# A latent attention lead-in in another order: the first four output tiles of the recurrent group stand ahead of head 0's projections, and the value weights are rounded behind head 0's squares

## The reference

```python
ob_l = mlstm_output(hb_l, pl[6], ml_head_gain[l])
...
q = (rms_norm(p[8], gq) @ w_uq).reshape(B, T, MLA_HEADS, MLA_NOPE + MLA_ROPE)
kv = (rms_norm(p[9], gkv) @ w_ukv).reshape(B, T, MLA_HEADS, MLA_NOPE + MLA_V)
k_nope, v = kv[..., :MLA_NOPE], kv[..., MLA_NOPE:]
...
q = rms_norm(q, qk_gain[0])
k = rms_norm(jnp.concatenate([k_nope, k_rope], axis=-1), qk_gain[1])
...
mix_l = jnp.concatenate([flat_heads(oa_l), ob_l, flat_heads(oc_l)], axis=-1) @ w_out[l]
```

## Time and profile before

| | |
|---|---|
| median of 3 runs | 2276.22 us (2275.09 to 2277.04) |
| the profiled execution: time, span | 2275.96 us, 2274.2 us |
| granted TensorE clock, mean over the span | 0.974 |
| TensorE matmul busy | 2104.3 us (93%) |
| VectorE, ScalarE, GpSimd busy | 1183.4, 751.0, 641.6 us |

### The profile page before, as it was taken

How to read it: one execution, slowest core, us unless ns; L and a number is a source line. 1 busy time by engine, 2 the same in 40 slices (tenths; PEclk the granted TensorE clock), 3 DMA queues, 4 the chain that set the end, 5 groups by cost and what they waited for, 6 DMA issues and landing times.

```text
span 2274.2 us, 30058 instructions
## 1 busy us (share of the span) xinstructions
PE 2104.3 (93%) x11774; PEld 1735.1 (76%) x11774; DVE 1183.4 (52%) x2119; ACT 751.0 (33%) x1221; POOL 641.6 (28%) x820
## 2 busy tenths in 40 slices
PE   6887999988889999999999988889988889999999
PEld 4576888866667888888888867778866658878887
DVE  4467613558874667166526566662358864212212
ACT  4234223456653311111111233322355644212222
POOL 1200311220002233333333421131221004555555
PEclk9999999999999999999999999999899989999999
DMA  7300332110002233233323210010111002223223
GB/s 283 102 7 32 120 116 83 38 37 19 10 10 66 75 112 121 84 112 112 102 94 120 85 57 19 19 58 29 47 38 37 10 10 71 96 93 97 97 93 102
DMA packets 76242, 165.58 MB, mean 73 GB/s; under 512 B 5192, under 2 KB 46664, under 8 KB 75088
## 3 DMA queue, kind: packets, MB, share of 16 engines
q1 hardware_dynamic: 75728, 163.28, 21.4%
q10 hardware_dynamic: 384, 0.47, 0.1%
HBM read 161.63 MB, written 2.10 MB: 72 GB/s over the span
## 4 chain that ended last, share of the span: by engine, by line
PE 79%; DVE 9%; ACT 5%; issue 5%; POOL 1%; DMA 1%; PEld 0%; SPq 0%; PEldq 0%; DVEq 0%; ACTq 0%; POOLq 0%
PE psum L1054 22%; PE psum L1056 21%; PE psum L1055 21%; PE psum L1613 1%; DVE naptlo L1986 1%; POOL wlo L517 1%; PE psum L1253 1%; PE psum L1136 1%; PE psum L1162 1%; DMA wm<-w_mod 1%; PE psum L1105 1%; PE psum L1382 1%; PE psum L1368 1%; PE psum L1319 1%; PE psum L1194 1%
## 5 line engine op out<-in xcount | busy, mean ns | idle before, releaser
L517 POOL TENSOR_TENSOR wlo<-raw,whi 128x256 fp32r<-128x256 f32 x816 | 641.4, 817 | 1624.5 <-ACT whi L542 1624.5
L1054 PE MATMUL psum<-hhi,whi 128*128 128x512 f32 (+1 forms) x1640 | 588.5, 359 | 24.9 <-DVEq L1813 12.6
L1055 PE MATMUL psum<-hlo,whi 128*128 128x512 f32 (+1 forms) x1640 | 580.1, 354 | 0.0
L1056 PE MATMUL psum<-hhi,wlo 128*128 128x512 f32 (+1 forms) x1640 | 580.0, 354 | 0.0
L542 ACT ACTIVATE whi<-raw 128x1024 fp32r<-128x1024 f32 x204 | 215.5, 1059 | 928.7 <-PE psum L1056 928.2
L1054 PEld LDWEIGHTS psum<-hhi,whi 128*128 128x128 f32 x1640 | 313.7, 191 | 75.6 <-issue 17.0
L1056 PEld LDWEIGHTS psum<-hhi,wlo 128*128 128x128 f32 x1640 | 313.0, 191 | 42.9
L1055 PEld LDWEIGHTS psum<-hlo,whi 128*128 128x128 f32 x1640 | 313.6, 191 | 40.8 <-issue 0.5
L2415 DVE TENSOR_TENSOR ffuf<-ffsa,psum 128x768 f32<-128x768 f32 (+1 forms) x44 | 36.1, 820 | 335.6 <-ACT ffsa L1005 328.9
L2400 DVE SCALAR_TENSOR_TENSOR ffmacc<-wm,csil,ffmacc 128x256 f32<-128x256 f32 x336 | 189.6, 605 | 10.4 <-DVE ffmacc L2400 5.3
L1054 PE MATMUL psum<-uhi,whi 128*128 128x512 f32 (+1 forms) x528 | 189.1, 358 | 2.6 <-DVE ulo L2419 1.5
(11 more groups left out here) (326 smaller groups left out, 3367.6 us busy)
## 6 DMA issues: line engine op xcount, KB each, us to landing
raw<-w_stream SPq DMA_DIRECT2D x204, 512.0 KB, 3.7
wm<-w_mod SPq DMA_DIRECT2D x80, 512.0 KB, 4.2
wm<-w_mod SPq DMA_DIRECT2D x8, 1024.0 KB, 17.7
xres<-x_t SPq DMA_DIRECT2D x8, 384.0 KB, 6.4
out<-xres SPq DMA_DIRECT2D x8, 256.0 KB, 2.2
consts<-c_f SPq DMA_DIRECT2D x1, 353.0 KB, 7.9
narpb<-rpb ACTq DMA_DIRECT2D x2, 120.0 KB
mlmask<-c_gate ACTq DMA_DIRECT2D x2, 108.0 KB
```

The source lines that it names most:

```text
L517: nc.gpsimd.tensor_tensor(wlo[:, q % 2, c:c + UW // 4], raw[:, q % RAW, c:c + UW // 4], whi[:, q % 2, c:c + UW // 4], ALU.subtract).then_i ...
L1054: mm(dst, ah, bh, start=first, stop=False)
L1055: mm(dst, ah, bl, start=False, stop=False)
L1056: return mm(dst, al, bh, start=False, stop=last)
```

## The change

TensorE does output tiles 0 to 3, all of unit 23, in one piece before `k_project(0)`. Before, tiles 0 and 1 stood there, tile 2 between `q_project(0)` and `q_sums(0)`, and tile 3 behind `k_sums(0)`. VectorE's `out_add` calls follow, ahead of `rope_key`, and so does the list of fills. ScalarE rounds unit 25 behind `q_square(0)` instead of behind `k_rsqrt(0)`. No instruction is added or taken away.

```diff
@@ lead_fills
-            return (out(0, 1, 2) + [("sumq", 0, x) for x in two] + [("sumk", 0, x) for x in range(2)] + out(3)
+            return (out(0, 1, 2, 3) + [("sumq", 0, x) for x in two] + [("sumk", 0, x) for x in range(2)]
@@ latent_act, lead_in
                     k_square(0)
                     q_square(0)
+                    his(u0(l, MA_V) + 1)
                     q_rsqrt(0)
                     k_rsqrt(0)
-                    his(u0(l, MA_V) + 1)
                     q_round(0)
                     k_round(0)
@@ latent_pe, lead_in
                     out_tile(0)
                     out_tile(1)
+                    out_tile(2)
+                    out_tile(3)
                     k_project(0)
                     q_project(0)
-                    out_tile(2)
                     q_sums(0)
                     k_sums(0)
-                    out_tile(3)
                     v_tile(0)
@@ latent_dve, lead_in
-                    out_add(0)
-                    out_add(1)
+                    for m in range(4):
+                        out_add(m)
                     rope_key()
-                    out_add(2)
                     q_scale(0)
                     k_scale(0)
-                    out_add(3)
                     v_lo(0)
```

## The result

The changed kernel takes 2262.41 us (median of 12 runs), the kernel before 2277.27 us in the same series. The ratio is 0.9932, 95% interval 0.9916 to 0.9948: 11.8 to 19.1 us off. In two later series it is 0.9938 (0.9918 to 0.9958) and 0.9943 (0.9924 to 0.9962); one execution of 8060.19 us, with a granted clock of 0.49, is left out of the first of these. The profiled execution took 2262.30 us, its span is 2260.5 us.

A forecast was written before the change was run, and what follows sets the result against it. TensorE, busy 93% of the span, was taken as the bound, losing time to idling or a lower clock. Earlier value tiles and clock, 7.0 + 5.2 + 0.6 = 12.8 us off, gave 2263.4 us; range 2259 to 2268.5.

The forecast's parts named there:

- Four output tiles in one piece, the gaps gone.: Ahead of the projections: waits of 0.76 and 1.97 us (layer 0) and 2.42 us (layer 1) vanish.
- The cover of `q_square(0)` gone.: `q_sums(0)` must wait for ScalarE's `q_square(0)`: new gaps of 1.1 us in layer 0, 2.2 us in layer 1.
- The rounding sets `v_tile(0)`.: Unit 25 rounded behind `q_square(0)`, then GpSimd's remainder: `v_tile(0)` starts 7.0 us (layer 0) and 5.2 us (layer 1) earlier.
- The slack of head 0's chain used up.: Layer 0: `k_scale(0)` moves by only 1.42 us, so `k_project(1)` waits 0 to 0.2 us for it.
- The clock: 0.6 us gained.: Value tiles: one half-rate stretch per lead-in again, 1.6 us in layer 0 (no gain), 2.0 in layer 1 (0.6 gained).
- Rival 1: Both lead-ins: the clock stays low from first gap through value tiles; only 7.9 us gained, 2268.3 us; chance 0.11.
- Rivals 2 and 3: Head 0's chain holds TensorE (2274.3 us, chance 0.04); tiles and rounding lengthen head 0's path (2281.8 us, chance 0.03).
- rival 2: Lead-ins: `k_scale(0)` or what follows ends last, so only 1.42 + 0.5 us count; 2274.3 us, chance 0.04.

The follow-up runs named there:

- second further step: On the changed kernel with ScalarE's three constant rows written later, unit 25 is also rounded ahead of `k_square(0)`; ratio 0.9924.
- Step 1 of the further steps: Against the changed kernel, ScalarE writes its three constant rows later in the lead-in, no longer ahead of `k_square(0)`; ratio 0.9913.

## Why the prediction was right

The forecast was 2263.4 us, 12.8 us off; 14.9 us off the median of 12 runs were measured, with 11.8 to 19.1 as the interval of the ratio. Its steps:

- *Four output tiles in one piece, the gaps gone.* Right. One thing was left out: between the end of unit 23 and `k_project(0)` TensorE lost 0.42 us to its own issue (8.82 us instead of 8.40). The mark that unit 23 is used up waits for its matmuls; before, that lay in the wait for unit 25. It made `q_sums(0)` 15.14 instead of 14.9 us; in layer 1 ScalarE's backlog hid it (11.99 against 12.0). The same 0.26 us of issue stand behind tile 3 where that tile is followed by the sums instead; no run took the mark away, so that it is the mark is argued.
- *The cover of `q_square(0)` gone.* Right: 0.90 and 1.73 us of wait, where 1.1 and 2.2 us of gap were given. The two figures count from different ends, the wait from the end of the last matmul, which lies 0.17 us behind the place where the next could start; in layer 1 the rest, 0.3 us, is the later start of `k_project(0)`.
- *The rounding sets `v_tile(0)`.* Right: 19.08 and 15.93 us against 18.9 and 16.2. Tiles without the rounding show that it is the rounding. The remainder took 2.78 us in both layers, not the 3.05 and 3.2 that I took. In layer 0 this made up for a rounding that began 0.4 us later than forecast, so 19.08 is nearer to 18.9 than the working deserves: that much is luck. On the rule of the Trainium skill (GPSIMD Engine Reference, Specifications): by it GpSimd and VectorE's instructions with two SBUF inputs contend. In this trace VectorE paid for it, and the remainder did not, since it was over before most of the rotation began; with the rounding first both paid (4.50 us for the remainder). The rotation's first instruction in layer 1, beside the remainder, took 1.04 us, and 0.69 us in layer 0, where the remainder was done:

```profile
1674.94 1.04 DVE L2213 TENSOR_TENSOR mart<-mar,marope 32x512 f32<-32x512 f32 x1
```

- *The slack of head 0's chain used up.* Right: `k_project(1)` starts at 475.46, 0.25 us behind the end of the value tiles' stream (474.98 + 0.23), and the step with the rounding first showed that this wait, and nothing else, then holds layer 0.
- *The clock: 0.6 us gained.* This term was mis-sized. The first three value tiles took 4.23 us instead of 5.83 in layer 0 and 6.20 instead of 6.84 in layer 1: 2.2 us gained, of which `scores(0, 0)` has 1.31 + 0.63 = 1.9 us, less by the wait of 0.25 us. I expected a stretch of half rate in each layer, and in layer 0 there was none in three profiles. The term also took one execution's clock for the kernel's: output tile 2's half rate, 1.57 us of the 6.90 in layer 0, was absent in the second profile of before. Against that profile the start of `v_tile(0)` in layer 0 gained 5.33 us where 7.0 was forecast, and the way from there to `scores(0, 0)` 1.1 us where nothing was. So the mechanism was right, and the total of 12.8 us is near the 12.6 and 14.3 us of the two comparisons in part by luck, since the two misses of the clock lie in opposite directions.
- *Rival 1* (half rate from the first gap through the value tiles, in both layers) came true in layer 1 in its mechanism, from the key's sums on, and not in layer 0. The 0.8 us that it priced for sums at half rate were not lost: `v_tile(0)` still had to wait 0.57 us for GpSimd behind them. *Rivals 2 and 3* did not happen; the mechanism of rival 2 is what the second further step ran into.

By the Trainium skill (TensorE: Matmul & The Clock Gate, HAM oscillation) a kernel whose short groups of matmuls each wait for data starts every group at the throttled clock, so that a wait is paid as idle time and again as slower work behind it. The runs agree for the long waits: those of 4.82 and 5.17 us were followed by half rate in both profiles of before. Step 1 of the further steps shows it for a shorter one: 1 us less of wait ahead of the sums came with 2 us less of half rate behind it.

## What to carry to other kernels

A weight buffer is given back by its last reader, so the last small piece of work on it decides when the next unit can be prepared. Finish such a unit in one piece, and put the preparation of the next in the first place on its engine where the buffer is free. Here the first alone brought nothing; the second alone was not tried. Then look for the chain whose slack the gain has used up, since the next step will meet it.

When an effect is not much larger than what the clock does to the rest of the program, compare distances inside the stage, from a mark that both kernels share, and take more than one profile of each.

## What the runs showed of the hardware

The half rate of 1.2 GHz fell in the same places of a lead-in in three profiles of one kernel, to 0.05 us, while the 1160 us between the lead-ins differed by 4.0 us in the same profiles and by 7.3 us between two of another order. In layer 1 it began behind a wait of 1.73 us ahead of the sums (1.72 to 1.73 us, in four profiles of four) and not where that wait was 0.68 us (none of four), even with one of 1.38 us behind the sums; in layer 0 waits of 0.90 and 1.09 us did not bring it in three profiles. Waits of 0.76 and 1.97 us had half rate behind them in two profiles of four, so waits of such a length don't decide it alone; behind the wait of 2.42 us it came in all four profiles that have it.

GpSimd's remainder took 2.78 us with VectorE mostly idle, 3.48 to 3.69 us beside `k_scale(0)` in before and with the tiles only and 4.50 us beside `rope_key`; VectorE's rotation beside it took 1.13 us an instruction instead of 0.68.
